# Renumbered expert rows in 8 KB runs, and token rows gathered as quarters and turned by VectorE, in a mixture-of-experts encoder step

## The reference

```
g_sel  = argmax(h @ w_rg + b_rg)                 # one of 4 groups for each token
e_val, e_idx = top_k(logits of that group, 2)    # 2 of its 8 experts
for each expert e, in blocks of its tokens:      # 32 experts
    hid = silu(xe @ w_gate[e]) * (xe @ w_up[e])  # w_gate, w_up: 1024 x 512 each
    yb  = hid @ w_down[e]                        # w_down: 512 x 1024
out[token] += gate * yb
```

## Time and profile before

| | us |
|---|---|
| median of 3 runs (lowest to highest) | 1135.36 (1135.23 to 1137.0) |
| profiled execution, span | 1135.8 |
| first matmul of the first item | 418.8 |
| end of the last item | 998.1 |
| TensorE busy | 1072.8 (94% of the span) |
| VectorE, ScalarE, GpSimd busy | 510.2, 499.9, 294.9 |
| HBM read and written | 261.2 and 37.5 MB |

### The profile page before, as it was taken

One profiled execution on the slowest core, in us unless ns is written; L12 is line 12 of the kernel. 1 busy time (PEld: TensorE's weight loads), 2 busy tenths in 40 slices (PEclk: granted clock), 3 DMA queues, 4 the chain that ended last, 5 costly groups with the idle time before them and its releaser, 6 DMA issues.

```text
span 1135.8 us, 17803 instructions
## 1 busy us (share of the span) xinstructions
PE 1072.8 (94%) x5270; PEld 613.2 (54%) x5271; DVE 510.2 (45%) x660; ACT 499.9 (44%) x683; POOL 294.9 (26%) x315
## 2 busy tenths in 40 slices
PE   5999996998999978999999999899999999999996
PEld 4899985876888633333333333233333333348884
DVE  5488999886232442123113123112311312277785
ACT  5445446664222224346336345334633635443332
POOL 2168776685000301011011101101101111023310
PEclk8999997999999889999999999899999999999998
DMA  8211952302123999989999999999999999966431
GB/s 269 66 56 38 274 149 75 104 33 93 56 100 111 355 358 399 371 319 351 395 398 360 398 396 360 396 398 370 355 395 399 357 398 396 402 245 203 169 130 42
DMA packets 149010, 299.28 MB, mean 263 GB/s; under 512 B 12000, under 2 KB 42752, under 8 KB 148971
## 3 DMA queue, kind: packets, MB, share of 16 engines
q1 hardware_dynamic: 134619, 263.64, 63.3%
q0 software_dynamic: 6512, 22.29, 5.7%
q10 hardware_dynamic: 7840, 12.85, 3.0%
HBM read 261.20 MB, written 37.54 MB: 263 GB/s over the span
## 4 chain that ended last, share of the span: by engine, by line
PE 53%; DMA 4%; issue 2%; SPq 1%; DVE 1%; ACT 1%; POOL 0%; ACTq 0%; DVEq 0%; POOLq 0%
PE ps_gate_up L2109 27%; PE ps_y L2122 14%; DMA raw_weights<-w_exp_up 3%; PE ps_gate L67 2%; PE ps_gate L69 2%; PE ps_gate L68 2%; PE ps_x L2091 2%; PE ps_h L2129 1%; SPq L85 1%; PE ps_h3t L2421 1%; DMA late_room<-y_rows,out_rows 1%; ACT weights L113 0%; PE ps_h3t L148 0%; POOL late_room L138 0%; DVE weights L113 0%
## 5 line engine op out<-in xcount | busy, mean ns | idle before, releaser
L2109 PE MATMUL ps_gate_up<-weights,x_turned 128*64 128x512 f32 x1568 | 352.0, 602 | 2.5 <-issue 1.7
L2109 PEld LDWEIGHTS ps_gate_up<-weights,x_turned 128*64 128x64 f32 x1568 | 110.3, 138 | 209.8 <-issue 209.8
L113 ACT COPY weights<-raw_weights 128x2048 f32 x93 | 174.4, 1899 | 106.9 <-issue 44.9
L113 DVE COPY weights<-raw_weights 128x2048 f32 x93 | 114.2, 1230 | 224.2 <-PE ps_gate_up L2109 86.0
L2122 PE MATMUL ps_y<-weights,h_turned 128*64 128x512 f32 x784 | 179.0, 598 | 0.9 <-ACT h_turned L2022 0.9
L461 POOL TENSOR_TENSOR conv_pool_taps<-conv_pool_taps,tap_product 128x448 f32<-128x448 f32 (+1 forms) x88 | 135.8, 1544 | 39.4 <-ACT tap_product L567 29.3
L122 POOL COPY token_ids<-item_tokens 128x1 int32 (+1 forms) x48 | 8.7, 181 | 451.2 <-PE ps_x L2091 451.2
L2061 DVE TENSOR_TENSOR hidden<-ps_gate_up,act_gate 128x256 f32<-128x256 f32 x49 | 20.8, 424 | 224.6 <-ACT act_gate L2013 212.4
L912 DVE SCALAR_TENSOR_TENSOR taps_bank<-a_ext,par,taps_bank 128x640 f32<-128x640 f32 (+1 forms) x128 | 101.5, 793 | 3.3
L2122 PEld LDWEIGHTS ps_y<-weights,h_turned 128*64 128x64 f32 x784 | 52.2, 136 | 93.3 <-issue 92.1
L567 ACT ACTIVATE tap_product<-a_ext,par 128x448 f32<-128x448 f32 (+1 forms) x104 | 75.4, 740 | 50.7 <-POOL conv_pool_taps L461 34.1
(11 more groups left out here) (292 smaller groups left out, 1555.0 us busy)
## 6 DMA issues: line engine op xcount, KB each, us to landing
raw_weights<-w_exp_gate SPq DMA_DIRECT2D x124, 512.0 KB
raw_weights<-w_exp_up SPq DMA_DIRECT2D x124, 512.0 KB
raw_weights<-w_exp_down SPq DMA_DIRECT2D x62, 1024.0 KB
y_rows<-y_tile ACTq DMA_DIRECT2D x96, 128.0 KB, 5.5
y_rows<-zero_rows SPq DMA_DIRECT2D x16, 512.0 KB, 6.1
x_rows<-x_tile SPq DMA_DIRECT2D x9, 512.0 KB, 2.6
h_rows<-h_tile SPq DMA_DIRECT2D x9, 512.0 KB, 2.9
late_room<-x_rows SPq DMA_DIRECT2D x9, 512.0 KB, 4.7
```

The source lines that it names most:

```text
L113: copy(S.work[s][:, :], raw).then_inc(S.w_ready[s], 1)
L2109: last = pe.matmul(ps_gu[side[j], :, :], x_t[:, c, side[of]], w[:, :, share(D_EXP, j)], start=(k == 0), stop=(k == KD - 1))
```

## The change

1. Gate/up rows are renumbered. Partition p now holds the 8 rows 8p to 8p+7. A piece is one matrix and one half of them: pieces 0 and 1 are gate and up with rows 8p to 8p+3, pieces 2 and 3 the other four. Four rows of 512 columns are one run of 8 KB, and one DMA of 1 MB loads a piece. Down pieces take two rows each (2p, 2p+1), also 8 KB. To fit this, `hidden` is written with even and odd columns apart.
2. TensorE needs pieces in pairs: `gate_up` waits for 0 and 1, then for 2 and 3, and frees them in pairs (`USED_AT`).
3. Token rows come as quarters: partition 32q + b holds quarter q (256 features, 1 KB) of tokens b and b + 32, by two indirect DMAs for each item. VectorE turns 32 x 32 blocks with two instructions (`turn_x`) straight into `x_turned`, after `hidden`; TensorE's 4 transposes, `ps_x` and ScalarE's copy are gone.
4. ScalarE copies piece 2 after the silu, not before it.
5. `routing` makes two lists of ids, by one more copy and two more matmuls on the way to `tokens_ready`; GpSimd prepares two tables for them.

```diff
-LANDED = (32, 32, 32, 32, 16, 16)
+LANDED = (16,) * len(PIECES)
+USED_AT = (0, 0, 1, 1, 2, 3)
 def piece_from(eng, S, s, dst, e, loaded):
     if s in GU:
-        rows = slice(2 * P * s, 2 * P * s + 2 * P)
-        for m in range(2):
-            eng.dma_start(dst.rearrange("p (k m n) -> p k m n", k=2, m=2)[:, :, m, :],
-                          S.w_experts[m][0, e, rows, :].rearrange("o (k p) n -> p (o k) n", p=P)).then_inc(loaded, 16)
+        h, m = divmod(s, 2)
+        src = S.w_experts[m][0, e, :, :].rearrange("o (p h c) n -> p (o h) (c n)", p=P, h=2)[:, h, :]
     else:
         first = 2 * P * (s - DOWN[0])
-        eng.dma_start(dst.rearrange("p (k n) -> p k n", k=2),
-                      S.w_experts[2][0, e, first:first + 2 * P, :].rearrange("o (k p) n -> p (o k) n", p=P))\
-           .then_inc(loaded, 16)
+        src = S.w_experts[2][0, e, first:first + 2 * P, :].rearrange("o (p k) n -> p (o k n)", p=P)
+    eng.dma_start(dst, src).then_inc(loaded, 16)
...
 def gather_tokens(pool, S, i):
...
-    pool.indirect_dma_start(out=S.x_tokens[:, :], out_offset=None,
-                            in_=S.h2_rows.rearrange("t (h n) -> (t h) n", h=SIDES),
-                            in_offset=bass.IndirectOffsetOnAxis(ap=ids, axis=0)).then_inc(S.x_gathered, 16)
+    for g in range(TURNS):
+        pool.indirect_dma_start(out=S.x_tokens[:, g, :], out_offset=None,
+                                in_=S.h2_rows.rearrange("t (q n) -> (t q) n", q=QUARTERS),
+                                in_offset=bass.IndirectOffsetOnAxis(ap=ids[g], axis=0)).then_inc(S.x_gathered, 16)
...
@@ routing, TensorE: before project(3, 0, (1,)) @@
+                pe.wait_ge(to_place, 4)
+                pe.wait_ge(quarters_set, 1)
+                for g in range(TURNS):
+                    last = pe.matmul(ps_ids[:, g, :], quarters[0:BLOCK, g, :], item_list[:, :], start=True, stop=True)
+                last.then_inc(placed, 1)
...
@@ experts, ScalarE @@
                     if not final:
-                        take(expert_of(act, i + 1), e, GU[0::2], i + 1)
-                    act.wait_ge(w_used[GU[3]], i + 1)
+                        later = expert_of(act, i + 1)
+                        take(later, e, GU[0:1], i + 1)
+                    act.wait_ge(w_used[USED_AT[GU[3]]], i + 1)
                     act.activation(act_g[:, :], ps_gu[:, 0, :], ACT.Silu).then_inc(silu_ready, 1)
                     if not final:
-                        leave_x(i + 1)
+                        take(later, e, GU[2:3], i + 1)
...
@@ experts, VectorE @@
+                def turn_x(i):
+                    dve.wait_ge(x_gathered, i * 16 * TURNS + 16 * TURNS)
+                    for g in range(TURNS):
+                        turn = dve.transpose(x_t[:, :, g * QUAD:(g + 1) * QUAD], x[:, g, :].rearrange("p (e c) -> p c e", c=KD))
+                    turn.then_inc(x_turned, 1)
...
-                    dve.tensor_tensor(hid[:, :], ps_gu[:, 1, :], act_g[:, :], ALU.mult).then_inc(hid_ready, 1)
+                    dve.tensor_tensor(hid[:, :].rearrange("p (c n) -> p c n", c=2), ps_gu[:, 1, :].rearrange("p (n c) -> p c n", c=2),
+                                      act_g[:, :].rearrange("p (n c) -> p c n", c=2), ALU.mult).then_inc(hid_ready, 1)
                     if not final:
+                        turn_x(i + 1)
                         take(later, e, GU[3:4], i + 1)
...
@@ experts, TensorE @@
-                for k in range(KD // SIDES):
-                    last = pe.transpose(ps_x[:, k, :], x[:, k * P:(k + 1) * P], S.ident[:, :])
-                last.then_inc(x_turned, 1)
...
                     gate_up(i, expert_of(pe, i))
-                    turn_x(i + 1)
                     down(i - 1, expert_of(pe, i - 1))
```

More of the change, by code:

```diff
@@ L109, in copy_piece @@
     eng.wait_ge(S.raw_loaded[s], n * LANDED[s])
-    eng.wait_ge(S.w_used[s], items)
+    eng.wait_ge(S.w_used[USED_AT[s]], items)
     raw = S.raw[:, bass.ds((n + 1) % 2, 1), s, :]
@@ L1559, in routing_tables @@
         pool.memset(t.tie_row[:, e:e + 1], float(FIRST >> e))
+        quarter = QUARTERS - 1 - e
+        pool.affine_select(out=t.own_quarter[:, :], in_=t.own_quarter[:, :], compare_op=ALU.is_ge, fill=float(quarter - 1),
+                           base=-quarter * QUAD, pattern=[[0, 1]], channel_multiplier=1)
         pool.affine_select(out=t.tie_col[:, :], in_=t.tie_col[:, :], compare_op=ALU.not_equal, fill=float(FIRST >> e),
@@ L1730, in list_tokens @@
                     for a in range(2 * T):
-                        for h in range(SIDES):
-                            last = pe.matmul(ps_items[h * BLOCK:(h + 1) * BLOCK, :], row_parts[j][:, a, :], at_item[:, :, a, :],
-                                             start=(j == 0 and a == 0), stop=(j == 1 and a == 2 * T - 1))
+                        last = pe.matmul(ps_items[0:BLOCK, :], row_parts[j][:, a, :], at_item[:, :, a, :],
+                                         start=(j == 0 and a == 0), stop=(j == 1 and a == 2 * T - 1))
                     return last
@@ L2032, in _ @@
                 act.sem_inc(y_stored, 16 * SIDES)
-                leave_x(0)
                 iteration(0, first=True)
@@ L2099, in gate_up @@
                         pe.wait_ge(S.first_loaded[0], sum(LANDED[s] for s in GU))
-                    for s in GU:
-                        if first:
-                            pe.sem_inc(w_ready[s], 1)
-                        else:
-                            pe.wait_ge(w_ready[s], e + 1)
-                        for k in (2 * s, 2 * s + 1):
-                            w = work[s].rearrange("p (k m n) -> p k m n", k=2, m=2)[:, k % 2, :, :]
-                            of, c = divmod(k, KD // SIDES)
+                    for h in range(2):
+                        pair = slice(2 * h, 2 * h + 2)
+                        for s in GU[pair]:
+                            if first:
+                                pe.sem_inc(w_ready[s], 1)
+                            else:
+                                pe.wait_ge(w_ready[s], e + 1)
+                        w = S.weights[:, pair, :].rearrange("p m (c n) -> p m c n", n=D_EXP)
+                        for c in range(KD // 2):
+                            k = h * (KD // 2) + c
                             for j in range(SIDES):
-                                last = pe.matmul(ps_gu[side[j], :, :], x_t[:, c, side[of]], w[:, :, share(D_EXP, j)],
+                                last = pe.matmul(ps_gu[side[j], :, :], x_t[:, k, :], w[:, :, c, share(D_EXP, j)],
                                                  start=(k == 0), stop=(k == KD - 1))
-                        last.then_inc(w_used[s], 1)
+                        last.then_inc(w_used[h], 1)
                 def down(i, e):
@@ L2497, in build @@
             S.g_ple_rows, S.b_ple_rows = (sb(n, [P, D], F32, early) for n in ("g_ple_rows", "b_ple_rows"))
-        S.work = [weights[:, s, :] for s in PIECES]
+        S.weights, S.work = weights, [weights[:, s, :] for s in PIECES]
         S.first_loaded = [whole.enter_context(nc.semaphore(f"first_{n}_loaded")) for n in ("gate_up", "down")]
```

75 lines of the change are left out of this document (40 added, 35 removed).

## The result

| | before | after |
|---|---|---|
| median of the runs, us (lowest to highest) | 1136.18 (1135.23 to 1138.28) | 1098.07 (1096.75 to 1100.92) |
| profiled execution, span, us | 1135.8 | 1096.3 |
| first matmul of item 0, of item 1, of item 48, us | 418.82, 432.00, 982.64 | 415.98, 426.93, 944.58 |
| end of the last item; from there to the end, us | 998.1; 137.7 | 960.0; 136.3 |

The ratio is 0.9665, 95% interval 0.9646 to 0.9683: 38 us faster, where 25.7 was forecast. The changed kernel ran on two more chips, unchanged, at 1100.4 us (0.9667) and 1101.7 us (0.9689), so the gain is 35 to 38 us.

What follows compares the result with a forecast made beforehand. TensorE was taken to bound the loop, leading the loads by 2.9 us in 92.5. Turns -27.7 and ring +2 gave -25.7, from 1135.8 to 1110 us; range for 8 in 10: 1100 to 1152.

Steps and rivals of the forecast that it cites:

- Direction and main mechanism: Whole loop: faster at 65%; TensorE stays the bound, its 8-item cycle 87.8 us against 86.7 of loads.
- 10.9 to 11.0: Sign that the forecast is right: TensorE's period per item in us, with no idle time ahead of gate/up.
- the price of the turn: TensorE's loop: dropping 4 transposes saves 0.59 us an item, 27.7 us over 47 items, period 11.56 to 10.97.
- the stall: Two late items near 720 us, 3.8 and 2.7 us too long, where three extra loads come in; left unchanged.
- the start: Routing up to the first matmul: 2 us of added work hidden, first turn between -1 and +1; value 0.
- the tail: Stages after the last item, held unchanged at 137.7 us.
- the ring: One-buffer x_tokens: turn, gather, next turn; 9.7 us, mean 10.9 with GpSimd held, against 10.97; charged 2 us.
- My sum by cycles: TensorE against loads over 5 experts and 8 items: 92.5 against 89.6 us before, 87.8 against 86.7 after.
- The rate: Weight loads in 8 KB runs: bounds 392 or worse to 421 GB/s, taken as 411.
- The landing: Second gather's arrival, counted from its own issue: 6.6 us taken, bounds 5.1 and 8.2.
- Rival A: The gather's ring becomes the bound; at a landing of 7.9 us, 28 us slower, 1164 us; chance 27%.
- the range: 8-in-10 range of the kernel's time, 1100 to 1152 us; low end has 411 surpassed and the stall gone.

Runs made afterwards that it cites:

- Experiment 3: Changed kernel plus a 16-column matmul between gate_up and down: 1113.88 us over 128 stationary columns, 1102.9 us over 64.
- Experiment 6: Changed kernel, ids copied before GpSimd's wait for the turn, three norm-row loads moved: behind the last expert 1097.47 us, spread over the loop 1092.63 us.
- runs_only: Kernel before with parts 1, 2 and 4 (gate/up runs 8 KB apart), one gather and TensorE's turn kept: 1134.59 us, ratio 0.9973.
- short_runs: Changed kernel with the old run lengths of 2 KB and 4 KB, so its output differs: 1116.89 us, ratio 0.9823.
- after_again: The changed kernel run again, unchanged, for comparison; span of its profiled execution 1098.9 us.
- early_ids_again: Second run of the changed kernel with ids copied before GpSimd waits for the turn: 1093.54 us beside the changed kernel's 1101.71.

## Why the prediction came out short

**Direction and main mechanism held.** TensorE set the pace: 25 of the 47 periods of the loop are 10.82 us, where nothing but its own blocks is left, and the loads stayed just under it. The measured period is 10.82 and not in the 10.9 to 11.0 that I named.

**The step that failed is the price of the turn.** The forecast was short by 13.8 us of span: 7.1 here, 5.3 in the stall, 5.0 in the start and 1.4 in the tail, less 5.0 that the ring took back. "Each item loses 4 transposes, 0.59 us from start to start, for 47 items in the loop: 27.7 us" measured 34.8. I priced a block at the distance to the next start, and took its neighbours as fixed; but the turn was a full-width block (128*128 in the earlier trace rows) between two half-width ones (128*64), and made both longer. Experiment 3 puts it on the width: the 0.10 at gate/up comes and goes with it, the 0.05 at down comes with it.

**The stall in the middle, "at its present price"**, gave back 5.3 us, together with the last item of the loop. My sum by cycles could not size it: at 418 GB/s a cycle loads in 35.65 / 0.418 = 85.3 us, 1.3 under TensorE's 8 x 10.82 = 86.6, less room than the 2.9 of before, and still the stall shrank. Experiment 6 shows that what is left of it is the three row loads. Parts 1, 2 and 4 together take most of it away (runs_only), and without the long runs, beside the faster TensorE, the pairs and the new order of the copies leave 17.33 us (short_runs); whether the runs do it without these was not tried. And 2.7 of the 5.3 was not a wait at all but the slow gate/up block behind the idle time, 9.78 us in the earlier trace rows: after the shorter waits of now it is 7.09.

**The rate.** From 392 and 411 I had 421 for 8 KB runs and took 411; it is 416 to 420. By the rule of the Trainium skill ("DMA: Bandwidth & Descriptors", section on why small descriptors are slow) the estimate is 3.5% from 2 KB to 8 KB; the rows give 392 to 418, 6.6%, so they differ in size and the measurement decides.

**The ring, +2**, cost 7.0. The landing was right (6.5 us; forecast 6.6, bounds 5.1 to 8.2). The turn is 1.17 us and not 0.9. What I left out is the copy of ids: I kept its 0.18 from the earlier trace rows, though it stands directly behind the turn and so beside VectorE's next copy; it takes 0.7 on average. With both, 9.7 becomes 10.5. The round shown has 11.26: over the 9.72 of my sum, 0.68 is the copy, 0.27 the turn, 0.30 the idle time of GpSimd between its two issues, which my sum hasn't got at all, 0.16 the held issue and 0.12 the step from the turn to the copy; the landing of that round is as forecast. Rival A's mechanism is real in 20 items, but 0.35 us long in each, and not the bound on average.

**The start, 0**, was -5.0 in this execution, and that is partly luck: without it the span would have been 1101.3 us, inside the range. ScalarE waited 6.34 us for the store instead of 7.20 and went on at 410.38 instead of 412.34, and the first matmul came 2.8 us earlier; in the changed kernel's other two profiles it starts at 415.9 and 416.5, and in the variants between 414.1 and 418.6. The other 2.2 is TensorE's clock. The windows 416 to 422 and 428 to 434 us of the changed kernel's profiled execution:

```profile
416.00:422.00 6.00, 6.00 (x22) 2.16 (x24) 0.69 (x1) 0.76 (x1) 1.96 (x3) 0.77 1.00 413
...
428.00:434.00 6.00, 6.00 (x31) 2.41 (x28) 1.23 (x1) 1.91 (x1) 1.92 (x2) 1.00 1.01 406
```

and of after_again:

```profile
416.00:422.00 6.00, 6.00 (x16) 1.88 (x18) 0.00 (x0) 0.00 (x0) 1.92 (x2) 0.51 1.00 411
...
428.00:434.00 6.00, 5.60 (x19) 2.13 (x21) 0.96 (x1) 0.49 (x3) 2.50 (x3) 0.72 1.01 408
```

The granted clock was 0.77 and then 1.00 in the one, 0.51 (the 1.2 GHz level nearly throughout) and 0.72 in the other (0.50 and 1.00 in the kernel before); items 0 and 1 took 10.95 and 10.81 us against 12.55 and 12.51. That is 3.3 us between two executions of one program, and the spans differ by 2.6 (1096.3 and 1098.9).

**The range** ended at 1100, for "411 surpassed and the stall at 720 gone"; the first came true and most of the second. The first measurement lies 1.9 us below it, the other two, 1100.4 and 1101.7, just inside. Errors of both signs made up the distance, the ring's 5.0 against the four others.

## What to carry to other kernels

Price a block that is to go by the period with and without it, and look at its neighbours: here a full-width TensorE instruction between half-width ones cost more than its own length. A one-buffer ring is to be summed with every link at the price that it has beside its new neighbour, the small copy behind the moved step too; and what doesn't depend on the end of the ring, as ids, goes ahead of the wait. Where two engines are within 2% of each other, a faster transfer pays by the stalls it removes, and the few extra loads in its queue are better spread over the loop (511.7 us against 513.5 for early_ids_again, though the whole times are not told apart).

## What the runs showed of the hardware

- The width of TensorE's instructions: a 16-column matmul cost 0.48 us over 128 stationary columns and 0.11 over 64, between blocks of 64.
- VectorE's 32 x 32 transpose of 128x256 float32: 627 ns reading every eighth element, 424 reading neighbours.
- Rates of this queue by run length: 392 GB/s at 2 KB, 411 at 4 KB, 416 to 420 at 8 KB, although 8 KB runs of a gate/up piece lie 16 KB apart.
- A copy of 128x2 ids on GpSimd took 0.18 us alone and up to 1.19 beside VectorE's copies.
- Small transfers in other queues landed later beside the longer runs: the gather after 6.5 us with 8 KB runs and 6.0 with short ones in the same kernel, stores of y after 6.6 against 5.9.
